# Three seven-product units instead of two per gate/up chunk, packed two plain groups apart

## The reference

```
h = h + 1/2 * SwiGLU(RMSNorm(h))           # block 1
h = h + concat([attention, rwkv]) @ W_out  # u = RMSNorm(h) @ W_in feeds both
h = h + 1/2 * SwiGLU(RMSNorm(h))           # block 2
swiglu(x) = (silu(x @ w_gate) * (x @ w_up)) @ w_down
# w_gate, w_up: 2048 x 5632, w_down: 5632 x 2048
```

## Time and profile before

| | |
|---|---|
| median of 3 runs | 1827.61 us (1827.36 to 1829.4) |
| the profiled execution | 1828.37 us, span 1826.6 us |
| granted TensorE clock, mean | 0.998 |
| DVE busy | 1505.4 us (82%) |
| ACT busy | 996.0 us (55%) |
| HBM read | 360.19 MB |

### The profile page before, as it was taken

How to read it: one execution, slowest core, us unless ns; L and a number is a source line. 1 busy time by engine, 2 the same in 40 slices (tenths; PEclk the granted TensorE clock), 3 DMA queues, 4 the chain that set the end, 5 groups by cost and what they waited for, 6 DMA issues and landing times.

```text
span 1826.6 us, 29757 instructions
## 1 busy us (share of the span) xinstructions
PE 1810.7 (99%) x10696; PEld 1538.4 (84%) x10696; DVE 1505.4 (82%) x1759; ACT 996.0 (55%) x1185; POOL 11.1 (1%) x23
## 2 busy tenths in 40 slices
PE   9999999999999999999999999999999999999998
PEld 7888888888888888999998888888888888888886
DVE  5888888888988986689967866688888888899996
ACT  7555555555555655755634655555555555555554
POOL 1000000000000000000000000000000000000000
PEclk9999999999999999999999999999999999999999
DMA  7767776777766678564433557677776777675664
GB/s 249 226 216 225 225 219 207 227 218 234 241 196 217 211 238 252 185 186 151 129 118 116 188 181 253 193 229 226 228 228 219 223 225 222 219 243 191 214 205 157
DMA packets 207853, 380.38 MB, mean 208 GB/s; under 512 B 16016, under 2 KB 35728, under 8 KB 207504
## 3 DMA queue, kind: packets, MB, share of 16 engines
q1 hardware_dynamic: 205616, 376.56, 65.1%
q10 hardware_dynamic: 1632, 2.50, 0.4%
q0 software_dynamic: 512, 0.06, 0.0%
HBM read 360.19 MB, written 18.87 MB: 208 GB/s over the span
## 4 chain that ended last, share of the span: by engine, by line
PE 95%; DVE 2%; ACT 1%; DMA 1%; issue 1%; SPq 0%; ACTq 0%; DVEq 0%
PE psB L428 31%; PE psA L428 30%; PE psB L1256 6%; PE psT L439 5%; PE psM L439 5%; PE psA L439 5%; PE psA L1256 4%; PE psB L439 3%; PE psM L428 1%; PE psA L1267 1%; PE psB L651 1%; DVE wlo L411 1%; DMA raw<-in_w_in 0%; DMA raw<-in_ffn_w_gate 0%; PE psT L1664 0%
## 5 line engine op out<-in xcount | busy, mean ns | idle before, releaser
L402 ACT CAST whi<-raw 128x1024 fp32r<-128x1024 f32 (+1 forms) x648 | 675.0, 1046 | 685.1 <-DVE raw L1487 188.5
L411 DVE TENSOR_TENSOR wlo<-raw,whi 128x1024 fp32r<-128x1024 f32 (+1 forms) x648 | 770.5, 1212 | 196.1 <-ACT whi L402 186.5
L428 PE MATMUL psA<-whi,xh 128*128 128x512 f32 (+1 forms) x572 | 219.5, 384 | 0.1
L428 PE MATMUL psA<-whi,xl 128*128 128x512 f32 (+1 forms) x572 | 219.1, 383 | 0.0
L428 PE MATMUL psA<-wlo,xh 128*128 128x512 f32 (+1 forms) x572 | 219.1, 383 | 0.0
L428 PE MATMUL psB<-whi,xh 128*128 128x512 f32 x544 | 211.7, 389 | 0.0
L428 PE MATMUL psB<-whi,xl 128*128 128x512 f32 x544 | 211.6, 389 | 0.0
L428 PE MATMUL psB<-wlo,xh 128*128 128x512 f32 x544 | 211.6, 389 | 0.0
L428 PEld LDWEIGHTS psA<-whi,xh 128*128 128x128 f32 x572 | 107.4, 188 | 21.3 <-DVE wlo L411 0.3
L428 PEld LDWEIGHTS psA<-whi,xl 128*128 128x128 f32 x572 | 107.3, 188 | 21.1
L428 PEld LDWEIGHTS psA<-wlo,xh 128*128 128x128 f32 x572 | 107.4, 188 | 21.1
(11 more groups left out here) (529 smaller groups left out, 3426.3 us busy)
## 6 DMA issues: line engine op xcount, KB each, us to landing
raw<-in_ffn_w_gate SPq DMA_DIRECT2D x176, 512.0 KB, 4.5
raw<-in_ffn_w_up SPq DMA_DIRECT2D x176, 512.0 KB, 4.6
raw<-in_ffn_w_down SPq DMA_DIRECT2D x176, 512.0 KB, 4.7
raw<-in_w_in SPq DMA_DIRECT2D x80, 512.0 KB, 3.5
raw<-in_w_out SPq DMA_DIRECT2D x32, 512.0 KB, 4.3
quads_dram<-stage SPq DMA_DIRECT2D x88, 128.0 KB, 4.1
stage<-quads_dram SPq DMA_DIRECT2D x22, 512.0 KB, 4.4
x<-in_x SPq DMA_DIRECT2D x4, 512.0 KB, 7.5
```

The costliest lines, as they stand in the source:

```text
L402: nc.scalar.copy(whi[:, slot, :, 0:ncol], raw[:, slot, :, 0:ncol]).then_inc(hi_ready, 1)
L411: nc.vector.tensor_tensor(wlo[:, slot, :, 0:ncol], raw[:, slot, :, 0:ncol], whi[:, slot, :, 0:ncol].bitcast(F32), ALU.subtract).then_inc(l ...
L428: mm = nc.tensor.matmul(ps[:, tb, 0:ncol], lhs[:, k0 + t, tok], rhs[:, slot, t, 0:ncol], start=(first and t == 0 and p == 0 and tb != open ...
```

## The change

A third unit in chunks 1 to 10 of both blocks. New order of a chunk: plain g = 0, 1; unit 0 at g = 2, 3; plain g = 4, 5; unit 1 at g = 6, 7; plain g = 8, 9; unit 2 at g = 10, 11; plain g = 12 to 15. `gate_up(n-1)` stands behind all of unit 0's DVE work instead of behind g = 3, and `turn_quads(n-1)` behind g = 4. The activation sums of the third unit are a second batch of half the width, with buffers of their own. In `unit_sums` the second and third addition change places, and ACT waits for three additions, not two, before it casts the up group.

```diff
-GATE_UNITS = 2
+GATE_UNITS = 3
+FIRST_SUMS = 2
-CHUNK = ([("gate", j) for j in (0, 1, 4, 5)] + [("unit", 0)] + [("gate", j) for j in (6, 7)] + [("up", 0)] + [("unit", 1)]
-         + [("up", j) for j in (1, 4, 5, 6, 7)])
+CHUNK = ([("gate", j) for j in (0, 1)] + [("unit", 0)] + [("gate", j) for j in (5, 6)] + [("unit", 1), ("gate", 7), ("up", 0)]
+         + [("unit", 2)] + [("up", j) for j in (1, 5, 6, 7)])
...
@@ ffn_load @@
-                        if g == 11:
+                        if g == 10:
                             quads_store(sp, f, n - 1)
@@ ffn_act, first_chunk @@
-                    if j == PER - 2:
+                    if j == PER - 3:
                         halves_hi(xh, xl_sum, x_sum_hi, x_sum, GATE_PAIR // 2, sum_number(f))
+                    if j == PER - 1:
+                        halves_hi(xh, xl_sum, x_sum_hi2, x_sum2, GATE_PAIR // 2 + 1, sum_number(f, gate=1))
@@ ffn_act, chunk and down @@
-                        nc.scalar.wait_ge(col_step, n * (4 * GATE_UNITS) + (4 * unit + 2))
+                        nc.scalar.wait_ge(col_step, n * (4 * GATE_UNITS) + (4 * unit + 3))
...
-                    nc.scalar.wait_ge(col_step, 4 * unit + 2)
+                    nc.scalar.wait_ge(col_step, 4 * unit + 3)
@@ unit_sums @@
             nc.vector.wait_ge(col_step, steps + (4 * unit + 1))
+            tt(col_sum[:, 1, :], col_sum[:, 0, :], raw[:, up, 1, :], ALU.add).then_inc(col_step, 1)
             tt(raw[:, up, 0, :], raw[:, up, 0, :], raw[:, up, 1, :], ALU.add).then_inc(col_step, 1)
-            tt(col_sum[:, 1, :], col_sum[:, 0, :], raw[:, up, 1, :], ALU.add).then_inc(col_step, 1)
-            nc.vector.wait_ge(col_step, steps + (4 * unit + 3))
+            nc.vector.wait_ge(col_step, steps + (4 * unit + 2))
             tt(col_sum[:, 2, :], col_sum[:, 1, :], raw[:, gate, 1, :], ALU.add).then_inc(col_step, 1)
@@ ffn_dve, first_chunk @@
-                    if j == PER - 3:
+                    if j == PER - 4:
+                        nc.vector.wait_ge(group_used, base + GD + GATE_PAIR + FIRST_SUMS)
+                        halves_dve(xh, xl, xl_sum, x_sum, GATE_PAIR // 2, sum_number(f))
+                    if j == PER - 2:
+                        halves_lo(xh, xl, xl_sum, x_sum_lo, x_sum_hi, x_sum, GATE_PAIR // 2, sum_number(f))
                         nc.vector.wait_ge(group_used, base + GD + GATE_PAIR + GATE_UNITS)
-                        halves_dve(xh, xl, xl_sum, x_sum, GATE_PAIR // 2, sum_number(f))
+                        halves_dve(xh, xl, xl_sum, x_sum2, GATE_PAIR // 2 + 1, sum_number(f, gate=1))
                     if j == PER - 1:
-                        halves_lo(xh, xl, xl_sum, x_sum_lo, x_sum_hi, x_sum, GATE_PAIR // 2, sum_number(f))
+                        halves_lo(xh, xl, xl_sum, x_sum_lo2, x_sum_hi2, x_sum2, GATE_PAIR // 2 + 1, sum_number(f, gate=1))
@@ ffn_dve, chunk @@
                         unit_lo(n, unit)
                         if j == 0:
-                            turn_quads(n - 1)
+                            gate_up(n - 1)
                     else:
                         split_lo(base, n, PER, g)
+                    if g == SLOTS:
+                        turn_quads(n - 1)
                     if g == 1 and not (isinstance(n, int) and n == 1):
                         turned_lo(n - 2)
-                    if g == SLOTS - 1:
-                        gate_up(n - 1)
@@ ffn_pe @@
-                        if j == 0 and isinstance(n, int):
-                            nc.tensor.wait_ge(act_lo_ready, sum_number(f) + 1)
+                        if j in (0, FIRST_SUMS) and isinstance(n, int):
+                            nc.tensor.wait_ge(act_lo_ready, sum_number(f, gate=j // FIRST_SUMS) + 1)
```

More of the change, by code:

```diff
@@ L192, in build @@
         prow = sb("prow", [P, P])
+        prow2 = sb("prow2", [2, P])
+        behind_rows = sb("behind_rows", [P, P])
         pcol = sb("pcol", [P, P])
-        prow2 = sb("prow2", [2, P])
         pcol2 = sb("pcol2", [P, 2])
@@ L285, in build @@
         col_lo = at("col_lo", [P, 3, COLS], col_sum, dt=F32R)
[L286 to L289, removed]
+        x_sum = at("x_sum", [P, 3, FIRST_SUMS, P], consts, plus=4 * P)
+        x_sum_lo = at("x_sum_lo", [P, 3, FIRST_SUMS, P], consts, plus=4 * P, dt=F32R)
+        x_sum_hi = at("x_sum_hi", [P, 3, FIRST_SUMS, P], consts, plus=4 * P + 12 * P * FIRST_SUMS, dt=F32R)
+        shares = at("shares", [P, TB, COLS], consts, plus=4 * P + 24 * P * FIRST_SUMS)
         xl_sum = at("xl_sum", [P, KD, S], xl)
         hl_sum = at("hl_sum", [P, KF, S], arena, plus=KF * S * 4)
+        x_sum_hi2 = at("x_sum_hi2", [P, 3, 1, P], prow, dt=F32R)
         token_scale = sb("token_scale", [P, S])
         same_r = sb("same_r", [P, P], F32R)
+        x_sum2 = at("x_sum2", [P, 3, 1, P], token_scale)
+        x_sum_lo2 = at("x_sum_lo2", [P, 3, 1, P], token_scale, dt=F32R)
         widx_scale = sb("widx_scale", [P, TB])
@@ L809, in unit_lo, with sum_number @@
             tt(col_lo[:, :, :], col_sum[:, :, :], col_hi[:, :, :].bitcast(F32), ALU.subtract).then_inc(col_lo_ready, 1)
-        def sum_number(f, b=None):
-            return f * (1 + (max(UNITS[0]) + 1) // 2) + (0 if b is None else b + 1)
+        def sum_number(f, b=None, gate=0):
+            return f * (2 + (max(UNITS[0]) + 1) // 2) + (gate if b is None else b + 2)
         def batch(b, f):
             if f is None:
-                return 2, slice(0, 2)
+                n = FIRST_SUMS if b == GATE_PAIR // 2 else GATE_UNITS - FIRST_SUMS
+                return n, slice(0, n)
             n = min(2, max(UNITS[f]) - 2 * b)
@@ L1101, in chunk @@
                             nc.tensor.wait_ge(act_ready, n + f * FC)
-                        if j == 0 and isinstance(n, int):
-                            nc.tensor.wait_ge(act_lo_ready, sum_number(f) + 1)
-                        unit_products(base, n, PER, g, (xh, xl), GATE_PAIR + j, (x_sum_hi, x_sum_lo), j, FIRST_UNIT[f] - GATE_UNITS + j,
+                        if j in (0, FIRST_SUMS) and isinstance(n, int):
+                            nc.tensor.wait_ge(act_lo_ready, sum_number(f, gate=j // FIRST_SUMS) + 1)
+                        sums = (x_sum_hi, x_sum_lo) if j < FIRST_SUMS else (x_sum_hi2, x_sum_lo2)
+                        unit_products(base, n, PER, g, (xh, xl), GATE_PAIR + j, sums, j % FIRST_SUMS, FIRST_UNIT[f] - GATE_UNITS + j,
                                       j == 0, j == GATE_UNITS - 1)
```

## The result

The changed kernel takes 1940.74 us (median of 4 runs, 1938.73 to 1945.31) against 1828.51 for the kernel before: ratio 1.062, interval 1.0607 to 1.0634. It is slower, as forecast, but by 112 us where I forecast 60 and set the upper end of the range at 1922.

The account below looks back on a forecast made before the run. PE, working without a gap, was taken as the bound; gate_up's circle and first-chunk stalls, less the saved work, add 26.1 us per block, +52.2, giving 1879.8; 8.5 for clock falls makes 1888 us, range 1864 to 1922.

Parts of the forecast that it names:

- The stall and its place: Before unit 0 in every chunk, PE waits 3.16 us for gate_up, which stands behind unit 0's DVE work.
- the path: From PE's end of a chunk's last unit through ACT and DVE to the next chunk's unit 0: 19.48 us.
- The period at full clock: From one unit 0 to the next: 25.16 us of PE work plus 19.48 gives 44.64 us, against 42.16.
- DVE's own waits: DVE waits about 1.4 us for PE before the additions of units 1 and 2.
- The first chunk: PE stalls 1.6 us for a late wlo, then 2.9 us before unit 0 of chunk 1, starting at 66.4.
- The second batch: First chunk, DVE: half-width activation sums for the third unit, between half and all of 3.07 us, taken as 2.0.
- Order of sums: In unit_sums, swapped additions delay col_hi some 0.3 us, hidden; in the down projection nothing, -0.1 to +0.3 each.
- The store at g = 10: SP store moves from g = 11 to 10, with turn_quads at g = 4 ahead of it: no effect.
- The failed step: Clock at half for 3.4 us behind one of four of the 20 long stalls: 5 x 1.7 = 8.5 us.
- the circle: Unit 0 to last unit on PE, then through ACT and DVE to the next unit 0: 44.64 us per chunk.
- the clock falls at every stall: Rival: all 20 long stalls bring half clock, 20 x 1.7 = 34 us on 1880, so 1914 us; chance 0.18.
- The range: Whole kernel: forecast's own 1870 to 1900 us, widened up to 1922 and down to 1864.

Follow-up runs that it names:

- The second experiment: Changed kernel with gate_up directly behind the four additions of unit 0, ahead of wlo of g = 2: 1840.74 us, ratio 1.0072.
- the third: Kernel before, two units, with unit 0 at g = 2, 3, unit 1 at g = 8, 9, gate_up behind unit 0's DVE work: 1885.21 us, ratio 1.0321.
- the stall filled: Changed kernel with 14 extra matmuls, results unused, before PE's wait for act_ready in each chunk: 1889.96 us, ratio 1.0339.
- the version that wins: Changed kernel with gate_up earlier, turned_hi later, close_gate's last addition behind wlo of g = 15, activation-sum batches moved: 1820.59 us, ratio 0.9958.
- the two-unit kernel: Kernel before, its two units moved to g = 2, 3 and g = 8, 9, gate_up behind unit 0's DVE work: 1885.21 us, ratio 1.0321.
- 3 matmuls: Changed kernel with 3 extra matmuls, results unused, before PE's wait for act_ready in each chunk: 1904.63 us, ratio 1.0421.

## Why the prediction was right or wrong

- **The stall and its place: right.** `gate_up` behind unit 0, 3.16 us forecast in every chunk, 3.2 measured at 20 of 20; the path 19.48 forecast, 19.48 measured from the end of the unit. The fit to the last digit is partly luck: wlo of g = 0 and 1 with hl took 0.18 less than forecast, and `gate_up` to the start of unit 0 0.16 more; the other links fit within 0.03. The second experiment shows the place to be the cause, the third that the third unit is not needed for it.
- **The period at full clock: 44.64 forecast, 44.99 measured** (changed kernel's first period, and all with the stall filled). The path isn't longer; PE's part is. From the start of unit 0 to the end of the last unit (68.06 to 93.55) it took 25.49 us for the 25.16 of 111 matmuls at 0.2267. Of these 0.33, 0.16 are the last matmul, whose record lasts 0.39 where starts are 0.2267 apart, and 0.13 are unit 0 itself, which takes that much longer than the other units, with the stall filled too (203.24 to 213.58, two plain groups with it, against 10.20). In 18 periods, 6 us.
- **DVE's own waits: half right.** Before the additions of unit 2 it waited 1.37 us, forecast 1.4. Before those of unit 1 it waited 1.8 us where no fall of the clock had followed the stall and 3.3 to 4.7 where one had, since they wait for PE to end unit 0.
- **The first chunk: 1.6 forecast, 1.7 measured; unit 0 of chunk 1 at 66.4 forecast, 68.06 measured.** DVE after the change (answering to the earlier trace rows):

```profile
50.89 1.23 DVE L416 TENSOR_TENSOR wlo<-raw,whi 128x1024 fp32r<-128x1024 f32 x1 [1.01 <-ACT whi L407]
...
53.24 0.28 DVE L1500 TENSOR_TENSOR xl_sum<-xh,xl 128x128 f32<-128x128 f32 x1
...
55.23 1.22 DVE L416 TENSOR_TENSOR wlo<-raw,whi 128x1024 fp32r<-128x1024 f32 x1
...
60.12 0.69 DVE L1500 TENSOR_TENSOR col_sum<-raw 128x512 f32<-128x512 f32 x1 [0.73 <-DMA raw<-in_ffn_w_up]
```

  The second batch took the 2.0 us that I chose. Missed were 1.0 us for ACT's cast of g = 14 and 0.7 for a landing: 3.3 us in two blocks. The trace before has the first at the same place, 1.03 us behind the batch of sums:

```profile
50.97 1.23 DVE L411 TENSOR_TENSOR wlo<-raw,whi 128x1024 fp32r<-128x1024 f32 x1 [1.03 <-ACT whi L402]
```

- **Order of sums: nothing, right** (1.0002, 0.9993 to 1.0012). The store at g = 10 was not tried alone.
- **The failed step: "I let the clock fall at one of four of the 20 long stalls: 5 x 1.7 = 8.5."** The mechanism, half clock behind a stall, paid inside the circle, was right; this term of the sum was mis-sized. The clock fell at 19, and the price per fall was wrong too: 2.8 us where it lasted 6.8. Measured in place of the 8.5: 51 us (1940.7 less 1890.0). The rival "the clock falls at every stall" had the number of falls nearly right and, at 34 us, the price wrong; it too ended short, at 1914. The rows that I had showed a single fall of 3.4 us after one wait, and I took its length for a constant. I then discounted it for dense work on both sides; here, with dense work on both sides, a stall of 1.6 us had no fall, but one of 3.2 had it 19 times in 20. That one wait is also no exception: it stands in all ten traces (2.9 or 3.0 us), and half clock for 3.4 us followed in nine of them. The Trainium skill ("TensorE: Matmul & The Clock Gate", "HAM oscillation — how this bites in real kernels") tells of a kernel whose matmuls wait some 3 to 5 us for a DMA before every next tile and start each of those at half clock. The changed kernel nearly agrees, 19 of 20 at 3.2 us; at 2.5 and 2.1 us only a part of the stalls did so, and at 1.6 none.
- **The range:** its lower end, 1870, doesn't follow from the terms named for it; 1879.8 without falls, less about 1 us for a shorter second batch, is 1879. The result lies above the upper end, so nothing hangs on it.
- **Added up** for block 1: unit 0 of chunk 1 is 1.7 us later than forecast, nine periods 0.35 longer each (3.2), and the clock costs 24.2 (426.06 for nine periods less 9 x 44.99, and 39.15 less 36.04 at the end). Forecast +26.1, with these +55.2; chunk 10 ended 533.27 - 478.11 = 55.2 us later. Block 2 is alike, and the span grew by 110.6.

## What to carry to other kernels

When a step is moved behind other work, follow the circle from the event that releases it to the event that it releases, through every engine's program order, and compare it with the bound engine's work along the same stretch; busy shares (DVE 83 to 89% of a period in the kernel that lost 112 us, 95% in the version that wins) don't show it. When such a circle leaves TensorE idle in each pass (here from 2.1 us on), price the clock as well, per stall and from runs at several lengths of stall, since it can cost as much as the stall. If a stall can't be removed at once, matmuls without use inside it tell its two prices apart.

## What the runs showed of the hardware that I had not expected

- The same idle time has different prices: 3.2 us idle cost 1.6 us more where half clock lasted 3.4 us, 2.8 where it lasted 6.8. The 16 long falls began 0.8 to 1.2 us before PE resumed; the short ones of the changed kernel 0.2 before, 1.1 and 1.3 after. From the third period of each block on, each long fall began 47.8 us after the last, the length of the period itself: falls and stalls keep step. Why the two lengths differ was not tested.
- Between 2.1 and 2.7 us idle only a part of the stalls has a fall (3 of 20 in the two-unit kernel, 9 of 20 with 3 matmuls), at 3.2 us nearly all (19 of 20), at 1.6 none. The length alone doesn't decide: the two-unit kernel's longest stall, 2.68 us, had none, a stall of 2.65 with 3 matmuls had one. What picks them was not tested.
- 280 matmuls without use made the kernel 51 us faster.
